# Attention in pairs of query tiles: one step for two tiles of a chunk, 256-key tiles two to a bank

## The reference

```python
# block 1, layer 0 ("block1"): 8 heads over shared keys, 8 heads with a bias and a neighbourhood
p = softmax(q @ k_all.T * scale)            # k_all: 256 context keys and 256 latent keys
y_lat = p @ v_all
y_ctx = softmax(q_ctx @ k_ctx.T * scale) @ v_ctx     # context queries see 256 keys
# block 1, layer 1 ("window"): 16 heads, latent queries only, a window mask and a sink
p = softmax(concat([q @ k_lat.T + mask, q @ k_ctx.T, sink]))
# block 2, layers 0 and 1 ("diff_0", "diff_1"): 8 heads, each the difference of two maps
a = softmax(q[0] @ k[0].T * scale) - lam * softmax(q[1] @ k[1].T * scale)
o = a @ v                                   # v is 128 wide; diff_0 has context queries too
```

## Time and profile before

| | us |
|---|---|
| median of 3 runs | 2625.24 |
| lowest, highest | 2623.75, 2627.37 |
| span of the profiled execution | 2627.1 |
| block1 in it | 110.7 |
| window | 77.0 |
| diff_0 | 85.9 |
| diff_1 | 47.6 |

### The profile page before, as it was taken

The page is one execution under the profiler, slowest core; times in us unless marked ns, Lnnn a source line. Parts: engine busy times, 40 slices in busy tenths (PEclk is TensorE's granted clock), DMA queues, the critical chain, the costliest instruction groups (busy, mean ns, idle before and its releaser), DMA issues.

```text
span 2627.1 us, 42629 instructions
## 1 busy us (share of the span) xinstructions
PE 2513.8 (96%) x16378; PEld 2102.4 (80%) x16378; DVE 1625.9 (62%) x2680; ACT 1290.2 (49%) x2420; POOL 250.8 (10%) x266
## 2 busy tenths in 40 slices
PE   7999999999998999999999999899999999999998
PEld 4855678889857998889886687688889999778887
DVE  2657565553687786668776763433326698775664
ACT  3356454433656764634336733422225644675653
POOL 3000100001202100314000001000002330011000
PEclk8999999999989999999999999999999999999999
DMA  7265522234555455534324535533236454634555
GB/s 281 88 226 184 192 96 96 96 87 136 169 172 190 166 181 171 172 107 153 113 96 145 157 121 180 198 98 97 92 94 175 156 177 163 197 119 137 186 176 150
DMA packets 125611, 393.64 MB, mean 150 GB/s; under 512 B 13776, under 2 KB 24016, under 8 KB 125328
## 3 DMA queue, kind: packets, MB, share of 16 engines
q1 hardware_dynamic: 123584, 386.47, 45.1%
q0 software_dynamic: 1872, 5.02, 0.7%
HBM read 390.39 MB, written 1.05 MB: 149 GB/s over the span
## 4 chain that ended last, share of the span: by engine, by line
PE 82%; DVE 7%; ACT 4%; DMA 3%; issue 2%; POOL 1%; SPq 0%; ACTq 0%; DVEq 0%; POOLq 0%
PE bank L635 21%; PE bank L637 21%; PE bank L636 21%; PE bank L632 4%; PE bank L683 3%; PE bank L818 2%; DVE w_low L1816 2%; PE bank L828 2%; PE bank L631 2%; PE bank L843 1%; ACT w_high L1128 1%; DVE smax L2083 1%; PE bank L841 1%; DMA ring<-in_w_down 1%; PE bank L778 1%
## 5 line engine op out<-in xcount | busy, mean ns | idle before, releaser
L1816 DVE TENSOR_TENSOR w_low<-ring,w_high 128x1024 fp32r<-128x1024 f32 (+2 forms) x604 | 689.9, 1143 | 528.6 <-ACT w_high L1128 525.5
L635 PE MATMUL bank<-h_high,w_high 128*128 128x256 f32 (+1 forms) x2832 | 958.6, 339 | 35.3 <-DVE h_low L2013 11.4
L637 PE MATMUL bank<-h_high,w_low 128*128 128x256 f32 (+1 forms) x2832 | 940.8, 332 | 0.0
L636 PE MATMUL bank<-h_low,w_high 128*128 128x256 f32 (+1 forms) x2688 | 892.4, 332 | 0.0
L1128 ACT CAST w_high<-ring 128x1024 fp32r<-128x1024 f32 (+2 forms) x604 | 576.1, 956 | 264.8 <-DMA ring<-in_w_down 150.5
L635 PEld LDWEIGHTS bank<-h_high,w_high 128*128 128x128 f32 x2832 | 540.7, 191 | 97.0 <-issue 24.3
L637 PEld LDWEIGHTS bank<-h_high,w_low 128*128 128x128 f32 x2832 | 540.7, 191 | 51.1
L636 PEld LDWEIGHTS bank<-h_low,w_high 128*128 128x128 f32 x2688 | 512.5, 191 | 49.9 <-issue 1.7
L635 PE MATMUL bank<-f_high,w_high 128*128 128x256 f32 (+1 forms) x616 | 194.6, 316 | 4.6 <-DVE w_low L1816 4.2
L637 PE MATMUL bank<-f_high,w_low 128*128 128x256 f32 (+1 forms) x616 | 193.0, 313 | 0.0
L636 PE MATMUL bank<-f_low,w_high 128*128 128x256 f32 (+1 forms) x528 | 168.0, 318 | 0.0
(11 more groups left out here) (281 smaller groups left out, 3303.4 us busy)
## 6 DMA issues: line engine op xcount, KB each, us to landing
ring<-in_w_up SPq DMA_DIRECT2D x176, 512.0 KB, 3.5
ring<-in_w_mod SPq DMA_DIRECT2D x112, 512.0 KB, 4.1
ring<-in_w_down SPq DMA_DIRECT2D x80, 384.0 KB, 3.1
ring<-in_w_down SPq DMA_DIRECT2D x80, 320.0 KB, 3.0
spare_slabs<-in_w_mod SPq DMA_DIRECT2D x48, 512.0 KB, 8.0
ring<-in_w_gate SPq DMA_DIRECT2D x48, 512.0 KB, 3.5
ring<-in_w_k SPq DMA_DIRECT2D x32, 512.0 KB, 3.5
ring<-in_w_v SPq DMA_DIRECT2D x32, 512.0 KB, 3.5
```

The lines of the kernel that those rows point to most:

```text
L635: pe.matmul(out, wh[:, cols], high, start=first, stop=False)
L636: pe.matmul(out, wh[:, cols], low, start=False, stop=False)
L637: ins = pe.matmul(out, wl[:, cols], high, start=False, stop=last)
L1816: v.tensor_tensor(wl[:, cols], raw[:, cols], wh[:, cols].bitcast(F32), ALU.subtract).then_inc(low_ready, 1)
```

## The change

`Attention` replaces the lists. Its items are pairs: query tiles 0 and 1 of a chunk, or 2 and 3. A pair with 512 keys is two "uses" of the banks, as two units were. A pair with 256 keys is one use: both tiles' scores lie side by side in a bank, one maximum instruction finds both tiles' maxima, and one copy moves both tiles' transposes.

Each engine's `attend` works through pairs. TensorE goes one pair ahead with the scores, then takes all transposes of a pair, all its slabs and all values of the pair before in one group each. In the head attentions the slabs now come behind the transposes, and ScalarE does the copies before the next pair's exps; in diff the old order stays. VectorE normalises pair j, finds the maxima of pair j + 1 and stores pair j - 2 (before: the unit before); in diff the store lies between the maxima of the next pair's two uses. The values of both tiles go side by side into bank 7, which is stored as 256 columns (two instructions in diff). A part of the modulation ends at pairs 5, 10, 15 in block1, 4 and 7 in window, 7 and 14 in diff_0. Finished chunks follow one step later, and more of them are left for behind the attention (`chunks_left`). The squares of the second context, which in window hung on finished chunks, hang on pairs 2 to 5.

Cut to its core (removed lines of the `attend` functions stand in the code above):

```diff
+        DIFF_PROBT = [HS[:, 6 + i, :] for i in range(2)] + [RS_[:, :], TMP[:, 1, :]]
+        HEAD_PROB = PROB + [SC[:, i, :] for i in range(2)]
+        HEAD_PROBT = [HS[:, 6 + i, :] for i in range(2)] + [SC[:, 2 + i, :] for i in range(4)] + [TMP[:, i, :] for i in range(2)]
         PAIR_SCORES = [bank[i] for i in (2, 3, 4, 1)]
...
+                self.pairs, self.diff, self.beside, self.ends = pairs, diff, beside, ends
+                self.sets, self.stores = (1, 2) if diff else (2, 1)
+                self.scores = DIFF_SCORES if diff else PAIR_SCORES
+                self.probt = DIFF_PROBT if diff else HEAD_PROBT
+                self.tiles, self.first, self.owner = [], [], []
+                for j, pair in enumerate(pairs):
+                    uses = [(0,), (1,)] if pair["T"] == TOK else [(0, 1)]
+                    self.tiles.append(uses)
+                    self.first.append(len(self.owner))
+                    self.owner += [j] * len(uses)
+                self.count, self.uses = len(pairs), len(self.owner)
...
+            def slabs(self, j):
+                done, start = 0, 0
+                for end in self.ends:
+                    if j < end:
+                        return done + 16 * (j - start) // (end - start)
+                    done, start = done + 16, end
+                return done
...
+            def copied(self, j):
+                return self.beside[self.ends.index(j)] if j in self.ends else None
...
+            "block1": Attention(pairs_of_heads(0, 4, 0, 0, (0, 2), None, False, True) +
+                                pairs_of_heads(5, 9, 4, P, (0, 2), lambda h, qt: BIAS[:, h, qt, :], False, False),
+                                False, BESIDE["block1"], (5, 10, 15)),
+            "window": Attention(pairs_of_heads(1, 0, 0, 0, (0,), lambda h, qt: MASKC[:, qt, :], True, True),
+                                False, BESIDE["window"], (4, 7)),
+            "diff_0": Attention(pairs_of_maps((0, 2)), True, BESIDE["diff_0"], (7, 14)),
+            "diff_1": Attention(pairs_of_maps((0,)), True, BESIDE["diff_1"], ()),
         }
-        AHEAD = 2
...
+        BRANCH_FROM = {"diff_0": 15, "diff_1": 1}
+        CHUNKS = {"block1": (2, 6), "window": (1, 4), "diff_0": (2, 6), "diff_1": (1, 5)}
...
+        def chunk_over(name, j):
+            per, last = CHUNKS[name]
+            return j // per if j >= 0 and j % per == per - 1 and j // per < last else None
...
+                def scores(j):
+                    pair = A.pairs[j]
+                    w = pair["T"]
+                    for s, tiles in A.of(j):
+                        if s >= 2:
+                            pe.wait_ge(ex_ready, e0 + 2 * s - 2)
+                        for x in tiles:
+                            first = tiles.index(x) * w
+                            for i, (q, k) in enumerate(pair["subs"][x]):
+                                ins = pe.matmul(A.scores[(2 * s + i) % 4][:, first:first + w], q, k, start=True, stop=True)
+                                if x == tiles[-1]:
+                                    ins.then_inc(sc_done, 1)
+                def turn(j):
+                    for s, _ in A.of(j):
+                        for i in range(2 - A.sets, 2):
+                            k = A.sets * s + i - (2 - A.sets)
+                            pe.wait_ge(pr_ready, t0 + k + 1)
+                            if k >= 2:
+                                pe.wait_ge(pt_ready, t0 + k - 1)
+                            src = A.prob(s, i)
+                            for t in range(TT):
+                                ins = pe.transpose(bank[5 + k % 2][:, t * P:(t + 1) * P], src[:, t * P:(t + 1) * P], IDENT)
+                            ins.then_inc(tr_done, 1)
...
+                def values(j):
+                    pair, uses = A.pairs[j], A.of(j)
+                    pe.wait_ge(pt_ready, t0 + A.sets * (uses[-1][0] + 1))
+                    if o0 + j:
+                        pe.wait_ge(o_ready, o0 + A.stores * j)
+                    last = pair["T"] // P - 1
+                    for s, tiles in uses:
+                        for x in tiles:
+                            cols = slice(x * P, x * P + P)
+                            for t in range(last + 1):
...
+                def modulation(j):
+                    for k in range(A.slabs(j), A.slabs(j + 1)):
                         if k and k % 16 == 0:
                             pe.wait_ge(rows_copied, n["rows"] + k // 16)
...
+                        mod_slab(A.beside[k // 16], k % 16)
+                scores(0)
+                for j in range(A.count):
+                    if j + 1 < A.count:
+                        scores(j + 1)
+                    if A.diff:
+                        modulation(j)
+                        turn(j)
+                    else:
+                        turn(j)
+                        modulation(j)
+                    if j:
+                        values(j - 1)
+                values(A.count - 1)
...
+                    for s, tiles in A.of(j):
+                        for i in range(2):
+                            act.wait_ge(nm_ready, m0 + 2 * s + i + 1)
+                            if A.diff and i == 0:
+                                if s >= 2:
+                                    act.wait_ge(pr_ready, t0 + s - 1)
+                            elif s >= 4:
+                                act.wait_ge(tr_done, t0 + A.sets * (s - 4) + (1 if A.diff else i + 1))
+                            for x in tiles:
...
+                def copy(j):
+                    for s, _ in A.of(j):
+                        for i in range(A.sets):
+                            k = A.sets * s + i
+                            act.wait_ge(tr_done, t0 + k + 1)
+                            if k >= len(A.probt):
+                                act.wait_ge(pv_done, p0 + A.owner[(k - len(A.probt)) // A.sets] + 1)
+                            nc.scalar.copy(A.probt[k % len(A.probt)], bank[5 + k % 2][:, :]).then_inc(pt_ready, 1)
...
+                exps(0)
+                for j in range(A.count):
+                    part = A.copied(j)
+                    if part is not None:
+                        mod_copy(part)
+                    if A.diff and j + 1 < A.count:
+                        exps(j + 1)
+                    if j == BRANCH_FROM.get(name):
                         begin(LIN["branch" + name[4:]], ahead)
...
+                    if not A.diff and j == A.count - 1:
                         begin(LIN[f"mix1_{vl}"], ahead, (0,))
...
+                    copy(j)
+                    if not A.diff and j + 1 < A.count:
+                        exps(j + 1)
+                    if between is not None:
+                        between(j)
+                    c = chunk_over(name, j - 3)
                     if c is not None:
...
+                        act.wait_ge(o_ready, o0 + A.stores * (j - 2))
                         finish(c)
...
-                if l == 0:
-                    mod_copy("2_0_2")
                 act.wait_ge(emptied["scalar"], LIN[f"group_{l}"].empty0["scalar"] + 4)
-                act.wait_ge(pv_done, n["unit"])
+                act.wait_ge(pv_done, n["pair"])
                 high_branch(4)
-                act.wait_ge(o_ready, n["unit"])
-                for h in range(7 - l, 8):
+                act.wait_ge(o_ready, n["stored"])
+                for h in chunks_left(f"diff_{l}"):
                     square_out(h)
...
+                def maxima(j, uses=slice(None)):
+                    pair = A.pairs[j]
+                    for s, tiles in A.of(j)[uses]:
+                        for i in range(2):
+                            dve.wait_ge(sc_done, e0 + 2 * s + i + 1)
+                            sc, at = A.scores[(2 * s + i) % 4], (4 * j + 2 * i + tiles[0]) % NS
+                            if pair["masks"] is not None:
+                                own.link(v.tensor_tensor(sc[:, 0:S], sc[:, 0:S], pair["masks"][tiles[0]][i], ALU.add))
+                            m = smax[:, at:at + len(tiles)]
+                            ins = v.reduce_max(m, sc[:, :] if len(tiles) == 1 else streams(sc[:, :], 2), AX_X, negate=True)
+                            if pair["sink"] is not None:
...
+                def store(j):
+                    dve.wait_ge(pv_done, p0 + j + 1)
+                    out = A.pairs[j]["out"]
+                    if not A.diff:
+                        v.tensor_copy(out, OUTB[:, 0:S]).then_inc(o_ready, 1)
                         return
...
+                    for x in range(2):
+                        r0 = srec[:, (4 * j + x) % NS:(4 * j + x) % NS + 1]
+                        v.tensor_scalar(out[:, x * P:x * P + P], OUTB[:, x * P:x * P + P], r0, None,
+                                        ALU.mult).then_inc(o_ready, 1)
+                maxima(0)
+                for j in range(A.count):
+                    normalise(j)
+                    if A.diff and j + 1 < A.count:
```

(36 more changed lines are left out.)

266 lines of the change are left out of this document (92 added, 174 removed).

## The result

The changed kernel takes 2636.3 us at the median (10 runs, 2629.4 to 2642.1), the kernel before, on the same chip, 2627.2 (10 runs): a ratio of 1.003, 95% interval 1.0018 to 1.0042. It is slower by 0.3%. The forecast was 2613.6, with 2602 to 2628 as its range: wrong in sign and outside the range.

A forecast was written before the change was run, and what follows sets the result against it. TensorE sets the pace in window, block1 and diff_0, VectorE in diff_1. Block1 -9.1, window +1.6, diff_0 -6.3, diff_1 +2.2 make -11.6: 2627.1 becomes 2615.5, less 1.9 for the median 2613.6 us; range 2602 to 2628.

The forecast's parts named there:

- The hand-over: TensorE's cost per group beyond its products: 0.62 to 0.66 us per unit, 0.48 in diff; fewer groups save 10.2 in block1.
- The waits for rows: TensorE's 1.15 us wait for copied rows at part ends goes: -2.3 us block1, -1.2 window, about -1.1 diff_0.
- A pair of window: Window: VectorE takes 8.27 us per pair against TensorE's 8.16 now, so nothing of the 5.1 saved is collected.
- From the last step to mix1_1: End of window: waits for mix1_1's weights and two late slab groups go, 8.5 us instead of 12.4, -3.9.
- Rival 4: TensorE's groups: the hand-over hangs on the weight loads and isn't saved, sum +6.3, 2631.5 us; chance 0.08.
- the wait for the fifth slab: Window's last three steps: the ring holds four slabs, so TensorE gets the fifth 2.25 us late.
- Each of these steps is then 1.9 scores + 2.2 transposes + 2.4 slabs + 2.25 wait + 1.9 values: Window's last three steps: 10.7 us each against 8.16, three make +7.8 us.
- Window's first steps, walked through with these durations, come 1.1 earlier: Start of window: its first steps come 1.1 us earlier, counted as -1.1 in window's sum.
- It fits, with at most 0.5 us late: Slab loads, up to four per step: 7.3 us needed, 5 to 6 between bursts, last needed 1.3 later.
- about 0.3 us late for each 512-key pair: Merged transposes: set 2 waits for the copy of set 0's bank; in block1 8 x 0.3 = +2.4 us.
- rival 2: Block1 and diff_0: Vector- and ScalarE's loop takes over through the one-pair lookahead; 8 us go, 2622, no change; chance 0.18.
- rival 3: Every burst waits for slabs, at TensorE's third and later slab of a step: about +22 us, 2636; chance 0.12.

The follow-up runs named there:

- the zeros: Against the changed kernel: 5 products that add zeros ahead of the fifth slab of window's last steps, 2 ahead of the sixth; 2631.8 us, 1.0021.
- the start alone: Against the changed kernel: only the first step's four slabs in window move ahead of the second pair's scores, the bursts stay; 2633.2 us, 1.0027.
- the bursts alone: Against the kernel before: units one by one, window's slabs four at every second unit, then 5, 5 and 6; 2643.2 us, 1.0067.

## Why the prediction was wrong

The span of the profiled executions grew by 10.0 where the forecast has -11.6. Of these 21.6, window has 10.2, block1 5.4, diff_1 2.9, diff_0 2.5, and about 0.5 lie outside. (The median missed by 1.1 more, since the forecast took it to lie 1.9 below the span, from three runs, and it lay 0.8 below.)

**What held.** The hand-over: 0.20 at scores, 0.12 at slabs, 0.15 at values were saved. By the rule quoted in the prediction from the Trainium skill (TensorE: Matmul & The Clock Gate, Part 3, The mechanism), as the prediction reads it, the same loads in fewer groups would save nothing; the trace disagrees with that reading by 0.7 us for each four units, in block1 and in diff_0 alike. The waits for rows are gone, in block1 with three waits of transposes for copies (0.57 each) that I had not counted; but the rows' waits there were 1.15 and 0.28, not "twice" 1.15. A pair of window took 8.13 to 8.65 where I had 8.27, though not by VectorE alone: in those two steps it was busy for 15.8 of 16.8 us, and TensorE for as long. From the last step to mix1_1 it was 8.9 where I had 8.5. Rival 4 is out.

**Window, forecast 78.6, measured 89.6.** The place of the loss was right, the last three steps, and so was the wait for the fifth slab: 1.9 to 2.5 against 2.25, all of them 7.8 against 6.8. Three steps took 39.6 against 32.1. (The prediction's sum of them is slightly off: three times 10.7 less 8.16 is 7.6, not 7.8.) The step that failed is "Each of these steps is then 1.9 scores + 2.2 transposes + 2.4 slabs + 2.25 wait + 1.9 values": it prices the products behind an idle time at full clock. In the trace of before the halved clock was there to read, behind the 1.97 idle us at the end of block1:

```profile
260.00:264.00 4.00, 4.00 (x12) 3.15 (x11) 1.22 (x1) 0.58 (x1) 0.00 (x0) 0.57 0.03 6
```

I had it and didn't carry it over. Of the 7.5 us, the zeros put 4.4 on the clock; 1.0 is in longer waits, 0.8 in transposes at 2.47 instead of 2.2. Most of the other 1.3 is in the slab groups themselves: a wait inside a group costs a hand-over too, 0.2 (five slabs of the second burst take 2.47 without their wait, where 5 x 0.43 and one hand-over make 2.27), and there are five such waits: 1.0. The last 0.3 stay open. At the start 2.8 are missing, 24.3 to the fourth pair's scores against the 21.5 that the forecast's terms leave for it: four waits of scores for exps, 2.94, 0.67, 0.54 and 0.57, where single units had slabs and transposes between their scores. (Read to the same points as above, the stage had 77.8 before, and 2.0 are missing. The clock is low at this start in both kernels: 0.57 from 742.11 to 750.04, and 0.52 from 742 to 752 in the kernel before.) "Window's first steps, walked through with these durations, come 1.1 earlier" was the step that failed there.

**Block1, forecast -9.1, measured -3.7.** Two terms. Waits for slabs, at "It fits, with at most 0.5 us late": 3.0 us in four waits, the longest 1.3 (1.6 to 3.9 in all in seven executions of this code). The loads' time to landing (min, median, max) in block1, changed kernel and before:

```profile
DMA to landing us min/median/max: 3.5/5.4/7.1
```

```profile
DMA to landing us min/median/max: 3.4/3.8/6.0
```

In bursts of three or four a load takes 5.4 at the median instead of 3.8. In the other traces the same code of the pairs has 4.9 to 5.6, single units have 4.4 in the run with window's bursts, and the pairs with slabs between the transposes 4.4 too: loads asked for in longer rows take longer, by 0.5 us or more. I had taken the time of a single load and the highest rate ever seen. Second, "about 0.3 us late for each 512-key pair": the wait is 0.33, as said, but a wait inside the group also costs the hand-over that merging was to save: the pair's transposes take 0.43 more than two single groups, where I had a wait of 0.3 less a gain of 0.15. That is 2.3 us more in eight pairs. Against them, 0.8 us more of old waits went than counted. The remaining 0.8 is again the slab groups with a wait inside, four of them, which take 0.2 to 0.5 more than their slabs and their wait. Other executions have block1 at up to 2.0 less, mostly by shorter slab waits. And the experiment with slabs between the transposes shows that neither could have been had back: behind them stood rival 2's ring.

**Diff_0, -6.3 and -3.8.** A head with four slabs takes 9.45 (1451.96 to 1461.41) instead of 10.18 (1457.33 to 1467.51 in the kernel before): 0.73 less, not 0.96, which is 1.8 in eight heads. At the start scores wait 0.85 more for exps. The two make 2.7 for a difference of 2.5; the rows' wait, 0.65 and not 1.1, is among the small terms.

**Diff_1, +2.2 and +5.1.** Of the 2.9 too few, 2.4 are the clock, which falls behind three idle times at pair 1. It is the same step that failed as in window: idle time priced by its length alone. With a clock of 1.00 the stage has 50.4 to 50.5, +2.7 to +2.8, near the forecast. The halving of weights, which I had left out of this stage since it was there before, makes these idle times at pair 1; wherever it stands, it costs about the same.

**The rivals.** The total is that of rival 3, 2636, and its place was right in kind. But its price was not: block1's slabs cost 3, not 20. That the total agrees is luck: most of the 22 us was really the clock in window and diff_1, the start of window and the missing part of the hand-over. I gave it 0.12 because one trace showed slabs on time when they came two by two; that trace said nothing about bursts. Rival 2's short lookahead showed at the starts of the stages, and inside block1 once the slabs were out of the way.

## What to carry to other kernels

Larger steps save hand-overs, but they also turn an even stream of loads into bursts: where one step takes more tiles than the ring holds, add a full load's time, less the work left in the burst, for each such step, and read the loads' time under the new pattern from the densest stretch, not from the quiet one. Price every idle time of TensorE with the clock behind it, not only with its length. Here the coarser step paid in the two long stages, in which products set the pace; in the two short ones its start, its end and its shorter lookahead ate up the gain (window without bursts) or more than that (diff_1). Decide stage by stage, and compare a stage over all executions in which its code is the same before a difference of 2 us is read as an effect.

## What the runs showed of the hardware

- An idle time of 1.9 to 2.6 us between full work was followed by TensorE's lower clock, 1.2 GHz, for 2 to 4 us in most cases, but not in all. Of the twelve first slab waits of window's bursts (the changed kernel, the start alone, the bursts alone, the halving at pair 4; 1.89 to 2.61), ten had slow products behind them and two didn't: 2.42 with the bursts alone and 1.89 with the start moved. In diff_1 waits of 1.76 and 0.46 and a third of 0.7 to 1.15 were followed by it in four executions and not in a fifth. Work that computes nothing in the same gap kept the clock at 2.4 GHz in all six bursts of the two kernels that had it.
- A 256-wide product with 6 columns of weights takes 0.43 us alone, and four of them, written to four quarters of a bank's partitions, also 0.43 (one slab). The Trainium skill (TensorEngine Tiling (Array Packing), Key Properties) says that tiles of the array work independently; the trace agrees, and it means that a slab's products can't be priced one by one.
